# Strassen's block products for the projections of a hybrid decoder trunk on Trainium2

## The chip, the cores and the metric

The kernel runs on the 8 cores of one Trainium2 chip. Each core takes half of one of the four sequences (1024 tokens) and computes both layers for it alone; nothing is exchanged between cores. The time is the device time of the slowest core, in microseconds, as the median of three runs.

## The reference, cut to what matters

```python
xn = rms_norm(h, norm_g)
proj = xn @ w_in                       # (tokens, 2048) @ (2048, 15360)
a_in, a_b, a_c, a_z, b_in, b_z, c_val, c_gate, c_z, gates = split(proj)
y_a = a_b * causal_dwconv3(a_c * a_in) * silu(a_z)
y_b = groupwise(trailing_mean_w(b_in) - b_in) * pool_scale * silu(b_z)   # w = 2, 4, 8, 16
v   = causal_dwconv31(c_val * sigmoid(c_gate)) + conv_c_b
y_c = silu(layer_norm(v)) * silu(c_z)
merged = sum over n of sigmoid(gates[n]) * (y_n @ w_branch_out[n])       # (1024 -> 2048) each
h = h + merged @ w_o
h = h + sigmoid(h @ w_ple_gate) * (p @ w_ple_proj)
# two such layers, then a final rms_norm
```

## The kernel before, in words

Channels lie on the 128 partitions, tokens along the free axis: `h`, `xn`, `acc` are 16 rows of 128 channels, `yb` eight. A core holds 1024 tokens and 62 earlier ones (`HALO`), which the causal convolutions need; the ranges `R_in` and `R_out` shrink from layer to layer: 1086, 1056, 1056 and 1024 columns, in matmuls of 362, 352, 352 or 512 columns (`R_L`, L149).

All work is recorded by one scheduler (`Sched`), which puts a semaphore wait on an instruction for each tile that it depends on. Each engine executes its list in the order of recording. Every instruction is issued from L134, so the profile tells them apart by tile, not by line.

A weight group is 256 output channels, loaded by a POOL DMA that casts to bf16 into one of two buffers (`load_main`, L280). `mm_group` (L301) runs the 16 contraction steps for one half of a group (128 channels) over all columns and rotates through the eight PSUM banks. After each half, one ScalarE or VectorE instruction reads the whole result: sigmoid, silu or copy on ScalarE, a product or a sum on VectorE.

The stages of a layer, in order: sums of squares through a matmul with ones, and `xn`; gate and value of branch C, whose product goes to the upper rows of `h` (bitcast to bf16); branch A; `merge_branch(0)` (L361: two gate groups, then four output rows of 8 steps each, four times over); branch B; `merge_branch(1)`; branch C, where mean and variance come from matmuls with ones and `cz_norm` (L502) normalises a row; `merge_branch(2)`; the projection `w_o` into `h`; the gate `w_ple_gate`, followed in each of its eight groups by the small product with `p` and the update of `h`. Six rows of `h` are reloaded before `w_o`, from `xT` in layer 0 and from `h_keep` in layer 1.

The 31 taps of branch C's convolution, 248 VectorE instructions a layer, are kept in a queue; `bg(n)` (L236) records the next n of them after a projection, and what is left is recorded ahead of branch C. In the last layer the squares for the final norm are summed by matmuls with ones inside the gate stage.

Of the kernel before, what the change touches and what calls it, by code (L numbers as in the profile page):

```python
# [9 lines left out]
F32 = mybir.dt.float32  # L10
# [11 lines left out]
HALO = 62  # L22
TOK = 1024
TL = TOK + HALO
NCORES = 8
# [118 lines left out]
class Rng:  # L144
    def __init__(self, lo, n, nt):
        assert lo + n * nt == TL and n <= 512
        self.lo, self.n, self.nt = lo, n, nt

R_L = [  # L149
    (Rng(0, 362, 3), Rng(30, 352, 3)),  # L150
    (Rng(30, 352, 3), Rng(62, 512, 2)),
]
R_FINAL = Rng(62, 512, 2)
# [3 lines left out]

def build_program(depth_run=DEPTH):
    nc = bass.Bass("TRN2", target_bir_lowering=False)
# [10 lines left out]
    h_keep = nc.dram_tensor("h_keep", [6 * 128, TL], F32, kind="Internal").ap()  # L170
# [3 lines left out]
    dma_names = ["x0", "x1", "x2", "x3", "par", "p", "hw0", "hw1", "hw2", "hw3", "hw4", "hw5", "hr0", "hr1", "hr2", "hr3", "hr4", "hr5", "ring0", "ring1", "side0", "side1", "out0", "out1", "out2", "out3"]  # L174
# [4 lines left out]
    def TT(out, in0, in1, op, reads, writes):  # L179
        S.op("dve", "tensor_tensor", dict(out=out, in0=in0, in1=in1, op=op), reads, writes)  # L180

    def TS(out, in0, s1, s2, op0, op1, reads, writes):
        kw = dict(out=out, in0=in0, scalar1=s1, scalar2=s2, op0=op0)
        if op1 is not None:
            kw["op1"] = op1
        S.op("dve", "tensor_scalar", kw, reads, writes)

    def STT(out, in0, scalar, in1, op0, op1, reads, writes):
        S.op("dve", "scalar_tensor_tensor", dict(out=out, in0=in0, scalar=scalar, in1=in1, op0=op0, op1=op1), reads, writes)

    def RECIP(out, in_, reads, writes):
        S.op("dve", "reciprocal", dict(out=out, in_=in_), reads, writes)

    def MM(out, lhsT, rhs, start, stop, reads, writes):
        S.op("pe", "matmul", dict(out=out, lhsT=lhsT, rhs=rhs, start=start, stop=stop), reads, writes)

    def DMA(eng, out, in_, reads, writes, sem):
        S.op(eng, "dma_start", dict(out=out, in_=in_), reads, writes, dma_sem=sem)

    with ExitStack() as es:  # L200
# [12 lines left out]
        Tt = ec(nc.sbuf_tensor("Tt", [128, 6, TL], F32))  # L213
# [448 lines left out]
```

How the kernel before makes its waits and increments, by code:

```python
                def body(eng, ops=ops, e=e):  # L105
# [15 lines left out]
                            todo.append((key, val))  # L121
                        emb = None
                        if o.meth is not None and not o.is_dma:
                            for t in todo:
                                if t[0][0] == "e":
                                    emb = t
                            if emb is not None:
                                todo.remove(emb)
                        for key, val in todo:
                            sem = dma_sems[key[1]] if key[0] == "d" else sems[key[1]]
                            eng.wait_ge(sem, val)
                        if o.meth is None:
                            continue
                        ins = getattr(eng, o.meth)(**o.kw)
                        if emb is not None:
                            ins._wait_ge(sems[emb[0][1]], emb[1])
                        if o.is_dma:
                            ins.then_inc(dma_sems[o.dsem], 16)
                        elif o.signal:
                            ins.then_inc(sems[e], 1)
```

## Time and profile before

| | |
|---|---|
| median of three runs | 2729.83 us (2727.36 to 2809.83) |
| profiled execution | 2733.91 us, span 2732.3 us on the slowest core (2721.1 to 2732.3) |
| granted clock, mean of each core | 0.981 to 0.986 |
| busy, share of the span | TensorE 96%, weight loads 54%, VectorE 49%, ScalarE 13%, POOL 8% |
| matmuls | 15074 recorded |
| weights loaded by POOL's queue | 188.82 MB, 53.7% of the DMA engines' time |
| median from issue to landing of 1 MB of weights | 10.2 us (`w_in`), 10.6 us (`w_o`) |

The busy shares say which engine could set the time; the windows by stage say whether it does so in that stage. The engines are separate, so a busy engine costs time only where another waits for it, and within an engine an instruction that waits holds back all that are recorded behind it.

### The profile page before, as it was taken

Reading aid. Unit: us, or ns where it says so; the run is one execution under the profiler, and the core shown is the slowest. Engines: PE = TensorE matmul, PEld = TensorE weight load, DVE = VectorE, ACT = ScalarE, POOL = GpSimd, SP = SyncE. Lnnn points to the kernel's source line nnn. Section 1 sums busy time; section 2 is a strip of 40 time slices with the busy share of each in tenths; the row PEclk is TensorE's granted clock in tenths of the full one; section 3 lists DMA queues with packets and bytes.
Section 4 is the critical chain, followed back from the end, with each engine's and each line's share of the span. In section 5 each row is a group of like instructions: output and inputs, shape, how many; then the busy total and the mean of one; then the engine's idle time right before and its main releaser. Section 6 shows DMA issues by size and latency. Waiting matters only on the chain.

```text
span 2732.3 us, 33287 instructions; the slowest of 8 cores (2721.1 to 2732.3 us)
## 1 busy us (share of the span) xinstructions
PE 2620.0 (96%) x15074; PEld 1474.3 (54%) x15168; DVE 1336.4 (49%) x1107; ACT 358.0 (13%) x335; POOL 213.6 (8%) x206
## 2 busy tenths in 40 slices
PE   3999999999999999999979999999999999999994
PEld 1566666666666666666646655544554444444442
DVE  3476676555762531212255666756467434221135
ACT  1000001101101311011120000110111022101111
POOL 0000000001000000001100000000100000000110
PEclk7899999999999999999989999999999999999997
DMA  7465565455645565566555556555565556556654
GB/s 166 47 78 70 70 77 71 69 80 66 86 65 85 79 94 72 68 78 85 68 90 66 74 78 78 74 76 76 72 79 79 82 74 107 77 71 74 89 70 141
DMA packets 353198, 218.62 MB, mean 80 GB/s; under 512 B 4000, under 2 KB 346016, under 8 KB 353056
## 3 DMA queue, kind: packets, MB, share of 16 engines
q0 software_dynamic: 345760, 188.82, 53.7%
q1 hardware_dynamic: 7296, 27.67, 3.1%
q8 instruction: 119, 1.95, 0.3%
q14 instruction: 23, 0.19, 0.0%
HBM read 393.55 MB, written 11.72 MB: 148 GB/s over the span
## 4 chain that ended last, share of the span: by engine, by line
PE 92%; DVE 4%; DMA 3%; ACT 1%; issue 1%; SPq 0%; DVEq 0%; ACTq 0%; POOLq 0%
PE psa L134 92%; DVE xn L134 1%; DVE Tt L134 1%; DMA par_s<-par 1%; ACT Tt L134 1%; DMA ring<-w_in 1%; DMA icnt_s<-icnt 0%; DVE h L134 0%; DVE yb L134 0%; DMA outT<-Tt 0%; SPq L134 0%; DVEq L99 0%; ACT L134 0%; ACTq L131 0%; DVEq L131 0%
## 5 line engine op out<-in xcount | busy, mean ns | idle before, releaser
L134 PE MATMUL psa<-xn,ring 128*128 128x352 bf16 (+2 forms) x11459 | 1969.3, 332 | 36.0 <-DVE xn L134 24.2
L134 PEld LDWEIGHTS psa<-xn,ring 128*128 128x128 bf16 x11520 | 1119.3, 98 | 880.6 <-DVE xn L134 42.5
L134 DVE SCALAR_TENSOR_TENSOR h<-h,par_s 128x1056 f32<-128x1056 bf16 (+1 forms) x480 | 624.1, 1300 | 13.1
L134 DVE TENSOR_TENSOR Tt<-psa,Tt 128x1056 f32<-128x1056 f32 (+2 forms) x128 | 159.2, 1244 | 713.9 <-PE psa L134 713.9
L134 ACT ACTIVATE Tt<-psa 128x1056 f32<-128x1056 f32 (+2 forms) x224 | 233.5, 1042 | 1808.0 <-PE psa L134 1781.1
L134 PE MATMUL psa<-yb,ring 128*128 128x352 bf16 (+1 forms) x1902 | 342.3, 338 | 1.0
L134 POOL DMA_DIRECT2D ring<-w_in x120 | 137.4, 1145 | 1700.4 <-PE psa L134 1672.0
L134 PEld LDWEIGHTS psa<-yb,ring 128*128 128x128 bf16 x1920 | 186.5, 97 | 153.0
L134 PE MATMUL psa<-acc,ring 128*128 128x352 bf16 (+1 forms) x1269 | 226.0, 338 | 0.6
L134 PEld LDWEIGHTS psa<-acc,ring 128*128 128x128 bf16 x1280 | 124.2, 97 | 102.0 <-issue 0.3
L134 DVE TENSOR_TENSOR h<-psa,h 128x1056 f32<-128x1056 f32 (+1 forms) x32 | 39.7, 1241 | 183.9 <-PE psa L134 183.9
L134 DVE TENSOR_TENSOR Tt<-Tt 128x1056 f32<-128x1056 f32 (+9 forms) x60 | 75.7, 1261 | 81.1 <-ACT Tt L134 79.7
L134 DVE TENSOR_TENSOR acc<-psa,Tt 128x1056 bf16<-128x1056 f32 (+1 forms) x32 | 39.7, 1241 | 128.3 <-PE psa L134 128.3
L134 DVE TENSOR_TENSOR acc<-acc,Tt 128x1056 bf16<-128x1056 bf16 (+1 forms) x64 | 79.5, 1242 | 2.2
L134 PE MATMUL psa<-Tt,ones_s 128*128 128x352 bf16 (+2 forms) x166 | 41.7, 407 | 40.0 <-ACT Tt L134 30.8
L134 DVE TENSOR_TENSOR yb<-Tt 128x1056 bf16<-128x1056 f32 (+1 forms) x32 | 39.7, 1242 | 63.7 <-ACT Tt L134 63.7
L134 DVE TENSOR_TENSOR h<-psa,Tt 128x1086 bf16<-128x1086 f32 (+1 forms) x16 | 20.4, 1274 | 102.3 <-PE psa L134 102.3
L134 ACT ACTIVATE xn<-h 128x1056 bf16<-128x1056 f32 (+1 forms) x32 | 34.2, 1070 | 222.7 <-DVE h L134 222.7
L134 ACT ACT_TABLE_LOAD x21 | 26.9, 1283 | 210.1 <-PE psa L134 197.0
L134 PEld LDWEIGHTS psa<-Tt,ones_s 128*128 128x128 bf16 x168 | 18.1, 116 | 61.4 <-ACT Tt L134 34.0
L134 DVE TENSOR_TENSOR Tt<-h 128x1086 bf16<-128x1086 f32 (+4 forms) x32 | 34.9, 1116 | 30.7 <-DMA h<-xT 28.8
L134 DVE SCALAR_TENSOR_TENSOR xn<-h,par_s,Tt 128x1086 bf16<-128x1086 f32 (+1 forms) x32 | 40.0, 1331 | 16.3 <-ACT Tt L134 16.3
(33 smaller groups left out, 422.4 us busy)
## 6 DMA issues: line engine op xcount, KB each, us to landing
ring<-w_in POOLq DMA_DIRECT2D x120, 1024.0 KB, 10.2
ring<-w_branch_out POOLq DMA_DIRECT2D x24, 1024.0 KB, 9.2
ring<-w_o POOLq DMA_DIRECT2D x16, 1024.0 KB, 10.6
ring<-w_ple_gate POOLq DMA_DIRECT2D x16, 1024.0 KB, 10.7
h<-xT SPq DMA_DIRECT2D x4, 2172.0 KB, 22.5
outT<-Tt SPq DMA_DIRECT2D x16, 512.0 KB, 4.5
h<-xT SPq DMA_DIRECT2D x6, 543.0 KB, 4.9
h_keep<-h SPq DMA_DIRECT2D x6, 543.0 KB, 9.2
```

Of the source, the lines that this page charges most:

```text
L134: ins = getattr(eng, o.meth)(**o.kw)
```

## The change

Every projection over 16 row chunks is computed by one level of Strassen's algorithm in Winograd's form. Contraction, output channels and tokens are each cut in two. For a group of 256 channels, seven products of eight matmuls replace eight.

- Tokens are stored in two halves (`HL`), blocks of 16 tokens going to the halves in turn; the host reorders inputs and output. `HALO` becomes 64. A matmul has 272 or 256 columns, or 512 in layer 1's `R_out`.
- Sums of weight quarters: `prep_a` makes three on VectorE (one in place, over the weights), `prep_b` one more there and a copy on ScalarE. They are recorded inside the last unit of the group before, if the group after is a fast one. Sums of token halves: `make_T`, four VectorE instructions for each of `xn`, `acc` and the bf16 copy of `h`, written over `h` or `xn`.
- A fast unit holds four banks. `part0`: one product, copied by ScalarE to a second bank. `part1`: three products; the first is copied to `m7`. `add0` and `add1` are VectorE adds from PSUM to PSUM. `tail0`, `tail1`, `tail2`: three products, recorded inside the *next* unit, so that the reads of a result (`evac`) and what follows it (`after`) come there too.
- `run_units` records unit by unit. `bg` records convolution taps while a clock kept for VectorE (0.17 us + elements / 960) is behind one kept for TensorE; both start at 0, and the squares and `xn` at the start count for VectorE only.
- Plain as before: `w_branch_out`, `pool_w`, `w_ple_proj`, the LayerNorm sums, and the first groups of the `xn`, `w_o` and `w_ple_gate` stages.
- A third weight buffer lies in `h` during the `w_in` stages and in `acc` during the gate stage. As `h` is overwritten, all 16 rows are reloaded before `w_o`; layer 0 writes all of them to `h_keep`.
- Squares for the norms are summed by ScalarE (`Square`) and VectorE (`square_sum`), then by one step of matmuls. `icnt` gets a semaphore of its own.

```diff
-R_FINAL = Rng(62, 512, 2)
+R_L = [((0, 34), (1, 33)), ((1, 33), (2, 32))]
+
+def _subs(R):
+    b, n = R
+    if n == 32:
+        return [(b, 32)]
+    return [(b, 17), (b + 17, n - 17)]
...
+    def bg(limit, most):
+        n = 0
+        while bgq and n < most and clock["dve"] < limit:
+            bgq.popleft()()
+            n += 1
...
+        def prep_a(g):
+            g.sb = state["sb"]
+            state["sb"] ^= 1
+            q, r = g.slot.quads, r_sb[g.sb]
+            TT(sb_ap(g, 0), quarter(g, 1, 0), quarter(g, 1, 1), ALU.add, [q[2], q[3]], [r[0]], 2)
+            TT(quarter(g, 1, 0), quarter(g, 0, 0), quarter(g, 1, 0), ALU.subtract, [q[0]], [q[2]], 2)
+            TT(sb_ap(g, 1), sb_ap(g, 0), quarter(g, 0, 0), ALU.subtract, [r[0], q[0]], [r[1]], 2)
+
+        def prep_b(g):
+            q, r = g.slot.quads, r_sb[g.sb]
+            TT(sb_ap(g, 2), quarter(g, 0, 1), sb_ap(g, 1), ALU.subtract, [r[1], q[1]], [r[2]], 2)
+            ACT(sb_ap(g, 3), quarter(g, 1, 1), AF.Copy, [q[3]], [r[3]])
...
+        def fast_unit(g, X, R, evac, after=None, last=False):
+            b, n = R
+            N = n * 16
+            u = Unit(g, 56 * (N / 2400.0 + 0.0035), evac, after, last)
...
+            def part0():
+                b0, b1, b2, b3 = u.banks
+                for bk in (b1, b2):
+                    if bits[bk] < N:
+                        mm(bk, 512, ones[:, :], ones_wide, True, True, [r_ones])
+                rhs, rr = xq(0, 0)
+                prod(b0, wq(0, 0), g.slot.quads[0], rhs, rr, True, True)
+                ACT(psa[:, b1, 0:N], psa[:, b0, 0:N], AF.Copy, [r_bank[b0]], [r_bank[b1]])
+
+            def part1():
+                b0, b1, b2, b3 = u.banks
+                rhs, rr = tq(2)
+                prod(b3, wq(1, 0), g.slot.quads[2], rhs, rr, True, True)
+                ACT(m7[:, u.m, 0:N], psa[:, b3, 0:N], AF.Copy, [r_bank[b3]], [r_m7[u.m]])
+                rhs, rr = xq(1, 0)
+                prod(b0, wq(0, 1), g.slot.quads[1], rhs, rr, False, True)
+                rhs, rr = tq(1)
+                prod(b1, sq(1), r_sb[g.sb][1], rhs, rr, False, True)
+
+            def add0():
+                b0, b1, b2, b3 = u.banks
+                TT(psa[:, b2, 0:N], psa[:, b1, 0:N], m7[:, u.m, 0:N], ALU.add, [r_bank[b1], r_m7[u.m]], [r_bank[b2]])
+
+            def tail0():
+                rhs, rr = tq(0)
+                prod(u.banks[1], sq(0), r_sb[g.sb][0], rhs, rr, False, True)
+
+            def add1():
+                b0, b1, b2, b3 = u.banks
+                TT(psa[:, b3, 0:N], psa[:, b1, 0:N], m7[:, u.m, 0:N], ALU.add, [r_bank[b1], r_m7[u.m]], [r_bank[b3]])
+
+            def tail1():
+                rhs, rr = tq(3)
+                prod(u.banks[2], sq(3), r_sb[g.sb][3], rhs, rr, False, True)
+
+            def tail2():
+                rhs, rr = xq(1, 1)
+                prod(u.banks[1], sq(2), r_sb[g.sb][2], rhs, rr, False, True)
...
+                        prep_a(u.group)
+                        prep_b(u.group)
+                    u.part0()
...
+                        evac(o, 0)
+                        bg(base + 0.55 * u.cost, 3)
+                        o.tail1()
+                        u.part1()
+                        o.tail2()
+                    else:
+                        u.part0()
+                        bg(base + 0.55 * u.cost, 3)
+                        u.part1()
+                release(u)
+                prep = prep and nxt.slot is not None
+                if prep:
+                    prep_a(nxt)
+                if o is not None:
+                    evac(o, 1)
+                if prep:
+                    prep_b(nxt)
+                state["old"] = u if u.fast else None
+                if not u.fast:
+                    for i in range(len(u.pieces)):
+                        evac(u, i)
+                look_ahead()
+                bg(clock["pe"], 4)
+            if state["old"] is not None:
+                finish(state["old"])
...
+        def square_sum(k, R, sq, r_sq, tot, r_tot):
+            src = ab(row(F_h, k), R)
+            if k == 0:
+                ACT(ab(tot, R), src, AF.Square, r_h[k], r_tot)
+                return
+            ACT(ab(sq, R), src, AF.Square, r_h[k], r_sq)
+            if k < 15:
+                TT(ab(tot, R), ab(tot, R), ab(sq, R), ALU.add, r_tot + r_sq, r_tot)
+            else:
+                TT(ab(view(ttb, 4 * 2 * TL, [[1, TL]]), R), ab(tot, R), ab(sq, R), ALU.add, r_tot + r_sq, r_T[4])
...
+                def pool():
+                    for c in range(2):
+                        src, r_src = Tt[:, c, :], r_T[c]
+                        lo, sh, st = R_in[0] * 32, 1, 0
+                        while sh < wlen:
+                            dst, r_dst = Tt[:, 2 + st % 2, :], r_T[2 + st % 2]
+                            lo += sh
+                            TT(dst[:, lo:TL], src[:, lo:TL], src[:, lo - sh:TL - sh], ALU.add, r_src, r_dst)
+                            src, r_src = dst, r_dst
+                            sh *= 2
+                            st += 1
...
+                    def norm():
+                        for c in range(2):
+                            i = 2 * j + c
+                            v = view(F_V, i * TL + LO, [[1, TL - LO]])
+                            TT(tmp[:, LO:TL], v, mu[:, LO:TL], ALU.subtract, [r_V[i]] + r_mu, r_tmp)
+                            TT(tmp[:, LO:TL], tmp[:, LO:TL], rstd[:, LO:TL], ALU.mult, r_tmp + r_rstd, r_tmp)
+                            ACT(tmp[:, LO:TL], tmp[:, LO:TL], AF.Silu, r_tmp + [r_par], r_tmp, bias=pcol(PB + 48 + i), scale=pcol(PB + 40 + i))
+                            TT(ab3(row(F_yb, i), R_out), tm3(tmp, R_out), ab3(row(F_T, s + c), R_out), ALU.mult,
+                               r_tmp + r_T[s + c], [r_yb[i]])
...
+                def ln():
+                    sl = slice(LO, TL)
+                    TT(tmp[:, sl], mu[:, sl], mu[:, sl], ALU.mult, r_mu, r_tmp)
+                    TT(rstd[:, sl], rstd[:, sl], tmp[:, sl], ALU.subtract, r_rstd + r_tmp, r_rstd)
+                    TS(rstd[:, sl], rstd[:, sl], 0.0, LN_EPS, ALU.max, ALU.add, r_rstd, r_rstd)
+                    ACT(rstd[:, sl], rstd[:, sl], AF.Ln, r_rstd, r_rstd)
+                    ACT(rstd[:, sl], rstd[:, sl], AF.Exp, r_rstd, r_rstd, scale=-0.5)
+                    n0()
+
...
+                    def gated(p, c=c):
+                        TT(P_ab(F_P, 2, p), P_ps(p), P_ab(F_P, c, p), ALU.mult, P_res(p) + r_P[c], r_P[2])
+
+                    def upd(oc=oc):
+                        TT(ab(row(F_h, oc), R_out), ab(row(F_h, oc), R_out), ab(row(F_P, 2), R_out), ALU.add, r_h[oc] + r_P[2], r_h[oc])
+                        if not last_layer:
+                            DMA("sp", h_keep[oc * 128:(oc + 1) * 128, :], h[:, oc, :], r_h[oc], [r_keep[oc]], f"hw{oc}")
```

In the gate stage a group's units are followed by two plain units (output rows c = 0 and 1), whose reads are `gated` and whose `after` is `upd`. In branch B the `after` of the first group is `pool`; in branch A the product `c_in` is followed by `conv3` (six VectorE instructions). In branch C the units in order are: the first z group, the mean (ahead of it the rest of the taps), the variance with `ln` as its `after`, three z groups with `norm`.

## Rows read from the trace of the kernel before

**Rows 1.** The page: busy by engine, the granted clock, the chain that ended last.

```profile
PE 2620.0 (96%) x15074; PEld 1474.3 (54%) x15168; DVE 1336.4 (49%) x1107; ACT 358.0 (13%) x335; POOL 213.6 (8%) x206
...
PEclk7899999999999999999989999999999999999997
...
PE 92%; DVE 4%; DMA 3%; ACT 1%; issue 1%; SPq 0%; DVEq 0%; ACTq 0%; POOLq 0%
```

**Rows 2.** Windows by stage: stretch, length, engines' busy us, clock, DMA share, GB/s.

```profile
101.20:427.90 326.70, 326.70 (x2112) 206.68 (x2113) 218.76 (x174) 23.70 (x22) 23.98 (x21) 0.99 0.56 71
601.10:729.20 128.10, 125.92 (x819) 78.82 (x817) 80.88 (x78) 18.30 (x17) 13.16 (x13) 1.00 0.55 71
902.40:970.20 67.80, 65.20 (x433) 41.77 (x432) 39.06 (x34) 26.01 (x23) 4.57 (x4) 1.00 0.57 87
1258.90:1394.40 135.50, 132.61 (x865) 82.78 (x864) 37.23 (x31) 19.11 (x19) 15.38 (x16) 1.00 0.61 86
1932.80:2055.40 122.60, 120.16 (x666) 65.06 (x673) 77.08 (x76) 17.89 (x17) 12.83 (x13) 1.00 0.58 73
2564.40:2696.00 131.60, 130.35 (x592) 58.45 (x604) 43.57 (x37) 24.82 (x24) 12.28 (x14) 1.00 0.51 64
```

**Rows 3.** Timeline of TensorE: start, length, instructions merged; merges of both layers.

```profile
471.21 29.03 PE L134 MATMUL psa<-xn,ring 128*128 128x352 bf16 x192
500.08 1.22 PE L134 MATMUL psa<-yb,ring 128*128 128x352 bf16 x7
...
1808.05 27.88 PE L134 MATMUL psa<-xn,ring 128*128 128x512 bf16 x126
1835.77 0.60 PE L134 MATMUL psa<-yb,ring 128*128 128x512 bf16 x2
```

**Rows 4.** Groups by form: count | busy us, mean ns of one | idle before, releaser.

```profile
L134 PEld LDWEIGHTS psa<-xn,ring 128*128 128x128 bf16 x11520 | 1119.3, 98 | 880.6 <-DVE xn L134 42.5 <-issue 9.8 <-DVE Tt L134 2.5
...
L134 DVE SCALAR_TENSOR_TENSOR h<-h,par_s 128x1056 f32<-128x1056 bf16 x232 | 305.6, 1317 | 6.3
...
L134 ACT ACTIVATE Tt<-psa 128x1056 f32<-128x1056 f32 x112 | 117.6, 1050 | 927.2 <-PE psa L134 900.4 <-DVE h L134 26.8
...
L134 DVE TENSOR_TENSOR Tt<-psa,Tt 128x1056 f32<-128x1056 f32 x64 | 80.4, 1256 | 368.0 <-PE psa L134 368.0
...
L134 DVE TENSOR_SCALAR Tt<-Tt,par_s 128x1056 f32<-128x1056 f32 x8 | 6.4, 801 | 0.3
...
L134 DVE TENSOR_TENSOR Tt<-h 128x1056 bf16<-128x1056 bf16 x4 | 2.7, 706 | 0.3 <-PE psa L134 0.2
L134 DVE TENSOR_TENSOR tmp<-Tt,icnt_s 128x16 f32<-128x16 f32 x16 | 2.7, 168 | 0.0
```

**Rows 5.** Timeline of ScalarE at the start, as rows 3.

```profile
51.02 1.17 ACT L134 ACTIVATE Tt<-psa,par_s 128x1086 f32<-128x1086 f32 x1 [11.31 <-DMA icnt_s<-icnt]
```

**Rows 6.** Windows around TensorE's wait for the third weight load, as rows 2.

```profile
98.00:101.20 3.20, 0.01 (x1) 0.05 (x2) 3.17 (x3) 0.00 (x0) 1.14 (x1) 0.83 0.33 41
101.20:103.00 1.80, 1.80 (x7) 0.90 (x8) 1.73 (x3) 0.00 (x0) 0.00 (x0) 0.50 1.39 117
103.00:106.00 3.00, 3.00 (x12) 1.49 (x11) 2.93 (x3) 0.00 (x0) 0.00 (x0) 0.50 0.86 84
```

**Rows 7.** Timeline of TensorE in layer 0's gate stage, two periods.

```profile
1292.71 14.61 PE L134 MATMUL psa<-xn,ring 128*128 128x352 bf16 x96
...
1309.65 1.53 PE L134 MATMUL psa<-xn,ring 128*128 128x352 bf16 x9
```

**Rows 8.** Timeline of ScalarE behind the variance, layer 0.

```profile
930.48 2.20 ACT L134 ACTIVATE Tt<-Tt 128x1056 f32<-128x1056 f32 x2 [4.44 <-DVE Tt L134]
932.70 1.28 ACT L134 ACT_TABLE_LOAD   x1
934.00 1.27 ACT L134 ACTIVATE Tt<-Tt,par_s 128x1056 f32<-128x1056 f32 x1
```

**Rows 9.** The page's DMA issues: KB each, median us to landing.

```profile
h<-xT SPq DMA_DIRECT2D x6, 543.0 KB, 4.9
```

More of the change, by code:

```diff
@@ new lines, in build_program, with load_ready @@
+        bits = [0] * 8
+        queue = deque()
+        units = []
+        groups_seen = set()
+        def load_ready():
+            while queue:
+                g = queue[0]
+                pick = next((f for f in free if f.phase is None or f.phase == g.phase), None)
+                if pick is None:
+                    return
+                free.remove(pick)
+                queue.popleft()
+                g.slot = pick
+                hold = r_h[11] if state["loads"] < 3 else []
+                state["loads"] += 1
+                if g.kind == "bo":
+                    dst = view(pick.ap, 0, [[512, 8], [1, 512]])
+                else:
+                    dst = view(pick.ap, 0, [[256, 16], [1, 256]])
+                DMA("pool", dst, g.src.rearrange("(k p) c -> p k c", p=128), hold, pick.quads, pick.sem)
@@ L296, in load_side @@
+        def load_side(g):
             s = state["side"]
             state["side"] ^= 1
[L298 to L308 removed]
@@ new lines, in build_program, with mm, add_unit @@
+        ones_wide = view(ones[:, :], 0, [[0, 4], [1, 128]])
+        def mm(bank, n, lhsT, rhs, start, stop, reads):
+            if start:
+                bits[bank] = n
+            S.op("pe", "matmul", dict(out=psa[:, bank, 0:n], lhsT=lhsT, rhs=rhs, start=start, stop=stop, skip_group_check=True),
+                 reads, [r_bank[bank]])
+        def add_unit(u):
+            units.append(u)
+            g = u.group
+            if g.kind in ("w", "bo") and id(g) not in groups_seen:
+                groups_seen.add(id(g))
+                queue.append(g)
+            return u
@@ new lines, in evac, with next_set, whole, finish @@
+        def evac(u, i):
+            u.evac(u.pieces[i])
+            if i == len(u.pieces) - 1 and u.after is not None:
+                u.after()
+        def next_set():
+            st = state["set"]
+            state["set"] ^= 4
+            return st
+        def whole(u):
+            u.place(next_set())
+            u.part0()
+            u.part1()
+            for i in range(len(u.pieces)):
+                evac(u, i)
+        def finish(o):
+            o.tail0()
+            o.add1()
+            evac(o, 0)
+            o.tail1()
+            o.tail2()
+            evac(o, 1)
+            state["old"] = None
```

842 lines of the change are left out of this document (499 added, 343 removed).

## The prediction

> **What bounds the kernel now.** I read the page first, then the spans by stage, then the order of instructions inside a stage. The page's shares and its chain of waits [rows 1] say that TensorE sets the time: it is busy for 96% of the span, holds 92% of the chain that ended last, and its granted clock stands at full speed in nearly every slice. The windows by stage [rows 2] say the same stage by stage: in the projections of layer 0 TensorE fills the whole stretch, in the pooling stage, the LayerNorm stage and the gate of the per-layer embedding all but 2 to 3 us. VectorE is busy for two thirds of the first stretch and a quarter to a half of the others, so today it is late nowhere for long. In the timeline of TensorE [rows 3] 192 products of 352 columns take 28.87 us from start to start (150.4 ns each) and 128 of 512 columns 27.72 us (216.6 ns): the columns at 2.4 GHz plus 3.5 ns. A weight group (256 output rows, 16 chunks) costs 14.43 us in layer 0 and 13.86 us at 512 columns.
>
> **The change, part by part.** All sums are against the profiled execution: span 2732.3 us, 2733.9 with what lies around it, 4.1 us above the median of the runs shown.
>
> *Columns.* 72 of each layer's weight groups become seven block products of eight matmuls. A group with two pieces of 272 and 256 columns costs 56 x (116.8 + 110.2) ns = 12.7 us, one of 512 columns 56 x 216.6 ns = 12.1 us: 1.7 us less each, 144 groups, **-248 us**. The branch outputs, the small projections and the first groups of three stages stay whole. The new matmuls are short; a weight load takes 98 ns here [rows 4], and no row shows one under fewer than 352 columns. I take it as hidden, since 98 is below 110; if half of the 52 ns between today's loads is needed too, 124 ns would stand against 110 to 117, some 10 ns in 10,080 short products: 0 to 100 us. The Trainium skill (TensorE: Matmul & The Clock Gate, section LDWEIGHTS) puts a load at its columns over 1.2 GHz, an estimate of 107 ns for 128; the row has 98, and by the one as by the other the sum stays, with 3 or 12 ns to spare.
>
> *Other work taken away.* The 32 matmuls that sum squares in the last gate stage go (7 us). The start no longer waits 11.3 us for icnt [rows 5] but gains a chain of squares and adds: -6. Two groups share the first pass over xn, whose rows come from VectorE every 1.3 us: -12 over both layers. A third weight buffer removes the 3.2 us gap and the clock at half level, 1.2 GHz, behind it [rows 6]: -5. The gaps in the five stages with side products or LayerNorm, 2 to 3 us of idle TensorE each [rows 2], and the filling of their short products go: -17. So if TensorE never waited longer than today: 2732 - 248 - 7 - 40 = **2437 us**.
>
> *What it adds to VectorE.* By size, VectorE costs 0.16 us + 1.04 ns a column, bf16 alone half the slope (706 ns at 1056); ScalarE 0.17 us + 0.84 ns [rows 4]. Added: 576 weight sums (0.69 us), 468 adds in PSUM (0.44 us at 272 columns, 0.69 at 512; no row has PSUM on both sides: lower bound this, upper bound twice it), 24 sums of tokens (2.4 us), some 80 more by split reads. That is 400 + 235 + 58 + 50 us on top of 1336: some 75% of the time, where it had 49%. The order of work matters more: a fast unit's last two products, and so its result, come only at the end of the *next* unit, and everything behind them on the in-order engines moves too. I follow five places; a product of eight matmuls is 0.93 us (1.73 at 512), its result is readable 0.26 us later.
>
> 1. *Gate of the per-layer embedding.* Now a period is 16.9 us [rows 7]. New, layer 0, from the end of the last gate unit: second sigmoid at 4.4; then on VectorE, in this order, the two gated reads 5.9, update of h 7.1, square on ScalarE 8.2, add to the running sum 9.6, weight sums 11.7 and 12.4, second gated read 13.9, update 15.1, square 16.2, add 17.5. The next group's second product needs the second weight sum (11.0), and ScalarE's copy of its first product stands behind the second square (16.6). After that TensorE still has 2 + 1 + 1 + 3 + 2 products: 24.8 us a period where its own work is 14.5. Cost 7 for the first and 6 x 10.3: **69 us**. Layer 1, counted the same way: 23.6 against 13.9, **65 us**.
> 2. *Pooling.* The pooled sums (2.6 us a level, 3.5 fixed: 6 to 14 us) can start only after the following unit, and the PSUM add of that unit queues behind them on VectorE. TensorE covers 5.4 us in layer 0, 3.5 in layer 1, where the pooling product itself waits: 30 + 28 us; the side products ahead of the next group's weight sums cost 2 us each, 17: **75 us**.
> 3. *LayerNorm of branch C.* Now the chain table load, Ln, Exp, table load, Silu [rows 8] runs under the next projections. New, the weight sums of the next group are issued *behind* that chain and both normalised rows: 18.8 us on VectorE and ScalarE, in which TensorE has one product. 19 + 18 us. The three later norms hold ScalarE's copies: 5.4 and 3.6 us each, 16 + 11. Squares through one buffer: 4 + 4. The planner also spreads 248 taps (1.32 us) by its own clock: in layer 0 it counts VectorE's start-up (50 us) as a lead, 50 + 410 of other work + 315 of taps = 775 us against 757 of TensorE, so 13 taps are left for the drain: 15 after what covers it. **86 us**.
> 4. *Three-tap convolution.* 6.9 us on VectorE (TENSOR_SCALAR 0.80, two of 1.32, twice [rows 4]) ahead of the next PSUM add; TensorE covers 5.4 and the lag of a tap adds 1.5. Layer 0 only, since at 512 columns it covers 10: **18 us**.
> 5. *Smaller.* First weight sums behind a branch output's reads in merges: 24 places, **29 us** (0 to 45). w_o: the bf16 copies of h stand ahead of ScalarE's copy, and two buffers for a load: **14 us** (0 to 30). The end: the last square is added on VectorE: **4 us**. The reload of h, 16 rows where 6 took 4.9 us each [rows 9], is counted at nothing: it runs under the last merge's final 14 us and the first three w_o groups (40 us); without that cover the ten late rows would cost 49 us, less what is left of it.
>
> *Clock.* After the 3.2 us gap the granted clock was 0.50, 1.2 GHz, for some 5 us [rows 6], 2.5 us lost. Places 2 to 4 make 15 gaps of that size: **37 us** (0 to 60).
>
> Sum: 2437 + 69 + 65 + 75 + 86 + 18 + 29 + 14 + 4 + 37 = 2834 us of span; 4.1 off and 1.6 on for the median: **2830 us**, 3.7% slower.
>
> **The rivals.** *A. TensorE stays the bound (faster).* Place 1 is the decider: if VectorE and ScalarE, a quarter idle or more, clear their queues before TensorE reaches the wait, only part of the 397 us is paid. For it: 248 us of columns are certain, TensorE has nothing else to wait for, and VectorE's idle time now is 1396 us. Against it: these waits are in the order of issue, not in the sum of work. With at most half paid: 2437 + 140 to 200, about **2600 us**; it wins wherever less than 240 us is paid. *B. Only the long chains hold (no change).* Places 1 to 3 without clock and small places: 2437 + 295 = **2732 us**. *C. VectorE becomes the bound of the first half (much slower).* Up to the drain it has some 775 us of work in layer 0 to TensorE's 750. If a PSUM add costs 0.9 us, 184 adds before it put 80 us more there, and as much again in layer 1: **2950 us**. It decides from 0.6 us an add. *D. The short products expose the weight load:* 2437 + 100 us and less waiting, since TensorE is later itself: about 2840, inside the forecast's range.
>
> **How the numbers follow.** A measurement tells 2% from no change here, 55 us. Forecast 0.46, D 0.05, A 0.25, B 0.18, C 0.06. The forecast's own range is 2760 to 2910 (chains 10% shorter or longer, small places at their bounds). The range reaches into A as far as half of it: 2620; above, to 2920. Faster by over 2%: A, 0.25. Within 2%: B and the lower edge of the forecast, 0.18 + 0.04. Slower: the rest of the forecast, C and D, 0.42 + 0.06 + 0.05 = 0.53.
>
> **What would show it.** TensorE's busy time near 2370 us and its count near 16,700. In the gate stages periods of 23 to 25 us, with TensorE waiting on VectorE's weight sums and on ScalarE's copy; if the period is below 18, A holds. One TensorE gap of 15 to 20 us a layer behind the variance product. In the pooling stage gaps that grow by 2.5 us from group to group. Weight loads of 98 ns with TensorE without gaps in the merges, where a group should take 12.7 us; 14 would be D. A PSUM add above 0.6 us would be C. The forecast is wrong if these waits together hold under 300 us.

## The result, and the profile after

The changed kernel took 2862 and 2867 us against 2727 to 2730 us before: ratio **1.0498 [1.0452, 1.0544]**, 5.0% slower, where 2830 us and 3.7% were forecast. In some runs cores ran long stretches at a lower granted clock; the slowest such runs are left out of the ratios, e5 and e8 are also compared by core 0 (its mean span over the runs in the ratio), and e7 is read by its undisturbed stages. The profiled execution took 2867.18 us, its span is 2865.6 us, 133.3 more than before.

The page after (busy by engine, granted clock in 40 slices, the chain that ended last), which answers to [rows 1]:

```profile
PE 2435.2 (85%) x16704; PEld 1649.2 (58%) x16704; DVE 2002.9 (70%) x2342; ACT 725.5 (25%) x1109; POOL 215.6 (8%) x206
...
PEclk9999999998997899998779999999999989999887
...
PE 65%; DVE 22%; ACT 5%; issue 5%; DMA 2%; SPq 0%; DVEq 0%; ACTq 0%; POOLq 0%
```

TensorE lost 185 us of busy time and gained 318 us of idle time. A quarter of the chain now belongs to VectorE and ScalarE, and yet neither is full. The windows by stage (length, busy us, clock), which answer to [rows 2]: first stretch, a merge, pooling, LayerNorm and gate of layer 0, then pooling, LayerNorm and gate of layer 1:

```profile
79.00:380.20 301.20, 288.37 (x2457) 240.75 (x2455) 242.53 (x321) 78.54 (x153) 27.57 (x23) 0.98 0.71 78
380.20:547.10 166.90, 159.56 (x1403) 136.03 (x1401) 148.18 (x170) 40.20 (x76) 11.79 (x11) 1.00 0.68 76
547.10:698.90 151.80, 121.55 (x973) 97.61 (x971) 113.83 (x156) 38.31 (x73) 12.93 (x13) 0.91 0.58 67
865.40:988.70 123.30, 77.16 (x583) 60.16 (x581) 83.31 (x93) 37.45 (x54) 5.45 (x5) 0.81 0.34 43
1265.80:1467.00 201.20, 141.51 (x1018) 107.50 (x1016) 91.68 (x116) 50.41 (x82) 13.07 (x14) 0.80 0.53 88
...
1952.50:2099.60 147.10, 120.05 (x716) 70.53 (x714) 113.33 (x143) 35.13 (x55) 12.92 (x13) 0.91 0.63 68
2259.50:2360.20 100.70, 69.97 (x286) 28.78 (x284) 60.17 (x65) 33.81 (x36) 5.50 (x6) 0.85 0.46 52
2636.40:2826.50 190.10, 132.61 (x509) 51.42 (x507) 86.34 (x88) 45.73 (x52) 10.75 (x12) 0.88 0.32 41
```

Stage by stage, in both traces (lengths in us; the cost is what the waits and the clock took, that is the difference plus the columns saved at 1.7 us a group and the small gaps that were there before). The w_o and gate stages are taken from first product to first product (in the changed kernel 1153.12, 1263.13 and 2521.85, 2633.79), the others from the windows, whose edges lie 1 to 8 us beside the first product of a stage:

| stage | before | after | cost, both layers | forecast |
|---|---|---|---|---|
| start, first stretch, change of layer, tail | 836.1 | 746.6 | 11 for the three-tap convolution | 18 |
| merges (three a layer) | 1018.8 | 977.6 | 42 | 29 |
| pooling | 128.1 + 122.6 | 151.8 + 147.1 | 80 | 75 |
| LayerNorm | 67.8 + 64.0 | 123.3 + 100.7 | 111 | 86 |
| w_o | 115.5 + 112.3 | 110.0 + 111.9 | 18 | 14 |
| gate | 135.5 + 131.6 | 203.9 + 192.7 | 164 | 134 |
| clock, forecast as a term of its own | | | in the rows above | 37 |

Pooling, LayerNorm and gate gave back more than the others won. (In the gate's 164 us are the 7 us of matmuls that went; the waits of LayerNorm's third norm, 5.39 and 4.29 us, stand in the merges' row.) The prices by form (count | busy us, mean ns), which answer to [rows 4]: the weight load, the PSUM add at two widths, a weight sum:

```profile
L135 PEld LDWEIGHTS psa<-h,sums 128*128 128x128 bf16 x4608 | 455.3, 99 | 200.3 <-DVE psa L135 21.2 <-issue 8.9
...
L135 DVE TENSOR_TENSOR psa<-psa,m 128x272 f32<-128x272 f32 x216 | 96.3, 446 | 148.6 <-PE psa L135 148.3
...
L135 DVE TENSOR_TENSOR psa<-psa,m 128x512 f32<-128x512 f32 x108 | 75.2, 696 | 162.4 <-PE psa L135 162.2
L135 DVE TENSOR_TENSOR ring<-ring 128x1024 bf16<-128x1024 bf16 x108 | 74.7, 692 | 3.7
```

They are near the forecast's (99 ns, 0.45, 0.70 and 0.69 us), so rival C falls. The merge, the second of the windows above, holds eight weight groups and four sets of branch outputs (14.5 us each by their columns): at 12.7 us a group that makes 8 x 12.7 + 4 x 14.5 = 159.6 us, and TensorE was busy for 159.56, so D, with 14 us a group, falls too. In the gate stage of layer 0 TensorE waits twice a period, first for the weight sums, then for ScalarE's copy of the first product (timeline of TensorE: start, length, idle before and its releaser):

```profile
1309.47 1.65 PE L135 MATMUL psa<-xn,acc 128*128 128x272 bf16 x8 [4.69 <-DVE acc L135]
1314.91 1.99 PE L135 MATMUL psa<-Tt,acc 128*128 128x272 bf16 x8 [3.79 <-ACT psa L135]
...
1336.59 1.46 PE L135 MATMUL psa<-xn,ring 128*128 128x272 bf16 x8 [4.68 <-DVE ring L135]
1342.03 2.00 PE L135 MATMUL psa<-Tt,ring 128*128 128x272 bf16 x8 [3.98 <-ACT psa L135]
```

These are the two waits of the forecast's place 1. The period is 1336.59 - 1309.47 = 27.1 us, where [rows 7] had 16.9 and the forecast 24.8. Windows of one such period say where the 2.3 us more are:

```profile
1305.00:1309.40 4.40, 0.00 (x0) 0.00 (x0) 3.22 (x5) 2.03 (x2) 0.00 (x0) 1.00 1.23 201
1309.40:1311.50 2.10, 1.65 (x8) 0.87 (x8) 2.03 (x5) 0.00 (x0) 0.00 (x0) 0.61 0.42 146
1311.50:1315.00 3.50, 0.09 (x1) 0.09 (x2) 2.26 (x3) 1.51 (x3) 0.00 (x0) 0.50 0.21 88
1315.00:1318.50 3.50, 3.50 (x16) 2.30 (x17) 0.86 (x1) 0.17 (x1) 0.00 (x0) 0.50 0.19 76
...
1322.00:1336.00 14.00, 9.37 (x82) 7.54 (x79) 5.56 (x8) 4.53 (x7) 1.87 (x2) 1.00 0.78 89
```

Behind the waits the granted clock is 0.50, 1.2 GHz, and a product of 272 columns lasts 1.65 to 2.0 us instead of 1.1. In LayerNorm of layer 0 the timeline of TensorE shows the drain, the wait of place 3 and the three norms:

```profile
899.82 1.06 PE L135 MATMUL psa<-h,ones_s 128*128 128x264 bf16 x4 [15.10 <-DVE h L135]
...
929.25 1.99 PE L135 MATMUL psa<-h,ring 128*128 128x272 bf16 x8 [15.79 <-DVE ring L135]
...
955.37 1.89 PE L135 MATMUL psa<-xn,ring 128*128 128x256 bf16 x8 [5.38 <-ACT psa L135]
...
994.97 1.89 PE L135 MATMUL psa<-xn,ring 128*128 128x256 bf16 x8 [5.39 <-ACT psa L135]
```

The forecast had 15, 19 and three of 5.4 us. ScalarE's chain [rows 8] is the same as before; what is new is that the weight sums stand behind it.

### The profile page after: what moved, and what is told of

It reads as the page before. It is cut to its first block, busy times and chain, and to the rows that moved or that the text cites. A ratio compares the mean times of both kernels' runs of the same rounds, so it can differ in the third digit from the quotient of the medians.

```text
span 2865.6 us, 39498 instructions; the slowest of 8 cores (2847.9 to 2865.6 us)
## 1 busy us (share of the span) xinstructions
PE 2435.2 (85%) x16704; PEld 1649.2 (58%) x16704; DVE 2002.9 (70%) x2342; ACT 725.5 (25%) x1109; POOL 215.6 (8%) x206
## 4 chain that ended last, share of the span: by engine, by line
PE 65%; DVE 22%; ACT 5%; issue 5%; DMA 2%; SPq 0%; DVEq 0%; ACTq 0%; POOLq 0%
PE psa L135 65%; DVE h L135 7%; DVE Tt L135 6%; DVE sums L135 3%; ACT Tt L135 2%; DVE acc L135 2%; ACT acc L135 1%; DVE psa L135 1%; DVE xn L135 1%; DVE ring L135 1%; DMA ring<-w_o 1%; DMA h<-xT 1%; DVE yb L135 1%; DMA outT<-Tt 0%; ACT psa L135 0%
## 5 line engine op out<-in xcount | busy, mean ns | idle before, releaser
L135 PE MATMUL psa<-h,sums 128*128 128x272 bf16 (+2 forms) x4608 | 705.4, 303 | 12.9 <-DVE psa L135 12.8
L135 PEld LDWEIGHTS psa<-h,sums 128*128 128x128 bf16 x4608 | 455.3, 99 | 200.3 <-DVE psa L135 21.2
L135 PE MATMUL psa<-xn,ring 128*128 128x272 bf16 (+2 forms) x3008 | 471.3, 304 | 70.0 <-DVE ring L135 35.7
L135 DVE TENSOR_TENSOR psa<-psa,m 128x272 f32<-128x272 f32 (+2 forms) x468 | 233.3, 499 | 420.9 <-PE psa L135 414.1
L135 PE MATMUL psa<-xn,sums 128*128 128x272 bf16 (+2 forms) x2544 | 422.0, 313 | 40.6 <-DVE psa L135 40.6
L135 ACT ACTIVATE Tt<-psa 128x544 f32<-128x544 f32 (+2 forms) x312 | 220.8, 708 | 837.0 <-PE psa L135 524.1
L135 PEld LDWEIGHTS psa<-xn,ring 128*128 128x128 bf16 x3008 | 297.3, 100 | 194.5 <-DVE ring L135 39.6
L135 PEld LDWEIGHTS psa<-xn,sums 128*128 128x128 bf16 x2544 | 255.3, 101 | 165.3 <-DVE psa L135 47.9
L135 PE MATMUL psa<-yb,h 128*128 128x256 bf16 (+2 forms) x1536 | 235.0, 310 | 13.7 <-ACT Tt L135 13.7
L135 PE MATMUL psa<-h,ring 128*128 128x272 bf16 (+2 forms) x1104 | 175.0, 302 | 39.6 <-DVE ring L135 39.4
## 6 DMA issues: line engine op xcount, KB each, us to landing
ring<-w_in POOLq DMA_DIRECT2D x88, 1024.0 KB, 12.7
```

What stands on the lines that cost most here:

```text
L135: ins = getattr(eng, o.meth)(**o.kw)
```

## The experiments

The theory: the time is lost in the order of issue on the in-order engines, behind the deferred tails, and in the half clock behind each such wait. The rivals: VectorE has too much work; the block products themselves are not worth their columns. All ratios are to the kernel before, measured beside it.

**e1: weight sums ahead of side products.**

```diff
-nxt = next((v.group for v in units if v.group is not u.group), None) if u.last else None
+nxt = next((v.group for v in units if v.group is not u.group and v.group.kind in ("w", "bo")), None) if u.last else None
```

> The work of every engine is the same; only the weight sums of the next weight group are issued earlier: in the last unit of the block-product group before, ahead of the side products and of the units of ones that lie between. Theory (the time is lost in the order of issue behind the deferred tails): a period of the gate stage loses the four sums that stand between its two gated reads, 2.8 us: 27.2 to about 24.5 us in layer 0, some 20 us a layer; the one TensorE wait a side product in pooling goes (8 us together), the 15.8 and 15.1 us waits behind the variance product shrink by 1 to 4 us only, because ScalarE's copy of the first product still stands behind the normalisation. Sum about 2815 us. Rival (the amount of VectorE work is the bound, its 2003 us at 70%): nothing was taken away, so 2865 us, periods still 27 us.

Measured: 2817 to 2827 us, ratio 1.0337 [1.0318, 1.0357]. VectorE's busy time is unchanged, 1999.8 us. In the gate stage the first wait is gone and the second has grown by less (timeline of TensorE, one period of 24.2 us):

```profile
1307.71 2.00 PE L135 MATMUL psa<-Tt,acc 128*128 128x272 bf16 x8 [6.54 <-ACT psa L135]
...
1331.88 2.00 PE L135 MATMUL psa<-Tt,ring 128*128 128x272 bf16 x8 [6.09 <-ACT psa L135]
```

That is 43 us for a change of order alone, where the rival of amount expected none.

**e2: dummy products in the gate's waits, first try.** Products of ones into the unit's next bank (`b3`) ahead of its first product from weight sums, and more of them (into `b2`) ahead of the product from `sums`.

> In the block-product groups 2 to 7 of the gate stages TensorE runs dummy products of ones (512 columns) where it waits: 20 and 15 of them a period in layer 0 (4.3 and 3.2 us for waits of 4.7 and 3.5 to 4.3), 15 and 10 in layer 1. Theory that the half clock behind these waits lengthens the period beyond the 24.8 us of the forecast: granted clock 1.00 through the period, products behind the waits 0.93 instead of 1.8 to 2.0 us, period 27.2 to 24.8 us in layer 0, about 1.2 us less in layer 1; together 20 to 25 us, 2842 us. Rival (the clock costs nothing because the waits behind it absorb it): clock 1.00, the waits longer by what the products gain, period still 27 us, 2865 us.

Measured: ratio 1.0629 [1.0592, 1.0667], slower. I had put the second batch behind the product that waits for ScalarE's copy, so it filled nothing; it ran at half clock and was added to the period, and the wait of 4.34 us left ahead of it still put the product behind it at 2.00 us (timeline of TensorE):

```profile
1316.60 2.00 PE L135 MATMUL psa<-Tt,acc 128*128 128x272 bf16 x8 [4.34 <-ACT psa L135]
1318.39 5.13 PE L135 MATMUL psa<-ones_s 128*128 128x512 bf16 x15
```

It says nothing on the question; e6 asks it again.

**e3: the gate's groups whole.**

```diff
-g = Group(w_pg[l][:, q * 256:(q + 1) * 256], "w", ph + 2, q > 0)
+g = Group(w_pg[l][:, q * 256:(q + 1) * 256], "w", ph + 2, False)
-    fast_group(g, X_h, R_out, sg)
+    plain_group(g, hrow, R_out, sg)
```

> The 14 block-product groups of the two gate stages are whole products again (the rest of the change stays). Theory (place 1 of the sum: the order of issue in these stages): periods back at about 17 us, the stages at 140 and 134 us instead of 201 and 190, so about 115 us less: 2750 us. Rival (amount of VectorE work): only 14 x 4 sums and 21 x 2 adds go, some 55 us of VectorE work, so at most 55 us less. Rival (nothing is lost here, block products cost little more than whole ones): TensorE has 25 us more columns to pass, so slower, 2890 us.

Measured: 2740 to 2743 us, 1.0042 [1.0026, 1.0058]: some 123 us less than the changed kernel, with 60 us less VectorE work (1942.7). A period is 16.7 us again. More than the amount rival's bound of 55 us came back, so the block products of place 1 alone made the difference between slower and no change.

**e4: e1, and the squares on the background queue.**

```diff
-square_sum(oc, R_out, row(F_P, 3), r_P[3], row(F_P, 4), r_P[4])
+bgq.append(lambda: square_sum(oc, R_out, row(F_P, 3), r_P[3], row(F_P, 4), r_P[4]))
```

> As e1, and in the gate stages the square and the add to the running sum of squares are no longer issued in the update of h but put on the queue of background work, which is issued behind ScalarE's copies of the next block-product group. All work is kept. Theory (order of issue): between the last sigmoid and the next group's copy VectorE has two gated reads and two updates, 5.4 us instead of 14; a period of about 18.5 to 20 us in layer 0 (TensorE's own 14.5 plus a wait of some 4), 18 in layer 1; gate stages about 147 and 140 us, together with the rest of e1 some 120 us less than after: 2745 us. Rival (amount of VectorE work): 2865 us, periods still above 26 us.

Measured: 2766 to 2777 us, 1.0157 [1.013, 1.0184], 20 to 30 us above the expectation: the adds to the running sum now stood ahead of the PSUM add, and TensorE waited for that (core 1; the next period has the same wait):

```profile
1306.53 1.10 PE L135 MATMUL psa<-xn,sums 128*128 128x272 bf16 x8 [3.58 <-DVE psa L135]
```

**e5: the squares behind the PSUM add.** As e4, but the closures go to a queue of their own that is emptied at the end of a block-product unit; even rows square into `F_T` row 4.

```diff
+while late and u.fast:
+    late.popleft()()
 look_ahead()
 bg(clock["pe"], 4)
```

> As e4, but the square and the add to the running sum are issued at the end of the next block-product unit, behind its PSUM add (in e4 they stood ahead of that add, and TensorE waited 3.6 us a period for it in layer 0 and 2.3 us in layer 1; even and odd rows get a buffer each). Theory (order of issue): that wait goes, and the half clock behind it; period about 16.5 to 17.5 us in layer 0 (e4: 20.5 to 22.2) and 15 to 15.5 in layer 1 (e4: 17.7); 50 us less than e4: 2720 us. Rival (amount of VectorE work): same work as e4, same 2770 us.

Measured: ratio 1.0085 [1.0019, 1.015]; the slowest core took 25 us or more above the expected 2720. Core 0's span, as a mean, is 2716.9 us, where e1 has 2814.7 and e4 2762.8: 46 us less than e4, where 50 were expected. In the gate stage of layer 0 a period is 15.8 us and the longest wait 0.5:

```profile
1317.02 1.10 PE L135 MATMUL psa<-xn,sums 128*128 128x272 bf16 x8 [0.43 <-DVE psa L135]
...
1332.78 1.10 PE L135 MATMUL psa<-xn,sums 128*128 128x272 bf16 x8 [0.43 <-DVE psa L135]
```

From 27.1 to 15.8 us with the same 1999 us of VectorE work: in layer 0 the order was nearly the whole of place 1. Layer 1's period is 17.6 us, where 15 to 15.5 were expected: two waits of 1.2 us stay.

**e6: the dummies in the right place, on the changed kernel.**

```diff
+for _ in range(u.warm[0]):
+    mm(b3, 512, ones[:, :], ones_wide, True, True, [r_ones])
 rhs, rr = tq(2)
 prod(b3, ...)
...
+for _ in range(u.warm[1]):
+    mm(b2, 512, ones[:, :], ones_wide, True, True, [r_ones])
 rhs, rr = xq(1, 0)
 prod(b0, ...)
```

> The test of the clock again, on the changed kernel itself, with the second dummies at their proper place: e2 put them behind the product that waits for ScalarE's copy, where they only added columns; here they stand ahead of it. 20 and 16 products of ones a period in layer 0 (4.3 and 3.5 us, in waits of 4.7 and 3.5 to 4.3), 15 and 10 in layer 1. Theory that the half clock behind the waits is what lengthens the period from the forecast's 24.8 to 27.2 us: granted clock 1.00 throughout, the three products behind the waits 0.93 us each instead of 1.8 to 2.0, period 24.8 in layer 0, about 1.2 us less in layer 1; together about 25 us: 2840 us. Rival (the waits are set by VectorE and ScalarE from a point that the clock does not move): period still 27 us, 2865 us.

Measured: 2832 to 2854 us, 1.0399 [1.0345, 1.0453]. The timeline of TensorE:

```profile
1329.99 1.10 PE L135 MATMUL psa<-xn,acc 128*128 128x272 bf16 x8 [0.37 <-DVE acc L135]
1330.93 3.62 PE L135 MATMUL psa<-ones_s 128*128 128x512 bf16 x16
1335.43 1.10 PE L135 MATMUL psa<-Tt,acc 128*128 128x272 bf16 x8 [0.89 <-ACT psa L135]
...
1354.58 1.10 PE L135 MATMUL psa<-xn,ring 128*128 128x272 bf16 x8 [0.37 <-DVE ring L135]
```

The window of this period, then one of the changed kernel's (length, TensorE, weight loads, VectorE, ScalarE, POOL, clock):

```profile
1329.99:1354.58 24.59, 22.80 (x164) 15.71 (x165) 12.12 (x17) 6.80 (x11) 1.87 (x2) 1.00 0.51 93
```

```profile
1309.47:1336.59 27.12, 18.11 (x129) 13.60 (x129) 12.13 (x17) 6.79 (x11) 1.87 (x2) 0.81 0.51 84
```

With TensorE kept at work the granted clock of this period is 1.00 and it lasts 24.59 us with the same work on VectorE and ScalarE; in layer 1 a period lasts 23.5 (TensorE's products behind ScalarE's copy start at 2729.65 and 2753.15). Those are the forecast's 24.8 and 23.6. So the chain of place 1 was counted rightly, and half clock is the rest. The dummies cover six periods a layer, (2.5 + 2.3) x 6 = 29 us, and the shorter runs, 2832 and 2836 us, are that much below the changed kernel's.

**e7: convolution and pooled sums in halves.** As e1; `conv3` and `pool` for one row chunk each, the second called between `add1` and the first read of the next group's first unit; z in two units in layer 1.

```diff
 o.add1()
+if o.mid is not None:
+    o.mid()
 evac(o, 0)
```

> As e1, and the three-tap convolution and the pooled sums are issued in two halves, one row chunk each: the second half stands behind the second PSUM add of the next group's first unit instead of ahead of it; in layer 1 the z groups of the pooling stage run as two units of 256 columns, so that they have a next unit to cover the halves. The work is the same. Theory (places 2 and 4: a long VectorE block ahead of a PSUM add): the four 2.8 us waits in layer 0's first stretch go (11 us); the waits of 1.9, 4.4, 7.2 and 9.8 us of layer 0's pooling fall to 4 us in all and those of layer 1 (3.5 to 10 us, 24 us in all) by half; with some half clock given back 40 to 50 us less than e1: 2775 us. Rival (amount of VectorE work): 2819 us, the waits only move.

Measured: ratio 1.0445 [1.0366, 1.0525]; nothing was won where 40 to 50 us were expected. The last pooling group of layer 0 had one wait of 9.78 us for VectorE and now has two that come to 10.07 (timeline of TensorE, first the changed kernel's, then e7's):

```profile
691.86 2.00 PE L135 MATMUL psa<-xn,sums 128*128 128x272 bf16 x8 [9.78 <-DVE psa L135]
```

```profile
681.26 1.10 PE L135 MATMUL psa<-xn,sums 128*128 128x272 bf16 x8 [2.85 <-DVE psa L135]
689.57 1.89 PE L135 MATMUL psa<-h,sums 128*128 128x256 bf16 x8 [7.22 <-DVE psa L135]
```

Between the two adds TensorE has one product of 1.1 us, which I had not counted, while VectorE has the second half of the sums: cutting a block in two does not shorten the chain from the last product of u to the first product that needs z's second add. The convolution's waits went from 2.80 to 3.16 us, for its read instead of its add. In places 2 and 4 halves did not help; the waits still grow from group to group with the length of the sums, as in the changed kernel (1.88, 4.52, 7.17 and 9.78 us).

**e8: LayerNorm's rows in pieces, planner level.** As e1; `norm` cut in a VectorE part and a ScalarE part, which go to a queue that is emptied behind the next units' copies and PSUM adds, and

```diff
 X_xn.make_T(R_in)
+if l == 0:
+    clock["dve"] = clock["pe"]
```

> As e1, and in LayerNorm's stage (place 3) the rows are normalised in pieces behind ScalarE's copies of the next block-product units, not in one block ahead of them (logarithm and exponential behind the first copy, then a row's subtraction and product at the end of one unit, its Silu and last product in the next); besides, the planner that spreads the convolution taps starts layer 0 with VectorE's clock equal to TensorE's, so that no taps are left over. The work is the same. Theory (order of issue): layer 0's waits of 17.8 (drain), 12.5, 4.6, 5.2 and 5.4 us fall to 5 us in all, layer 1's of 11.3 and three of 3.9 to 3 us; with 10 us of half clock given back about 70 us less than e1: 2750 us. Rival (VectorE is full in layer 0's first half): the drain's 15 us come back as waits between 80 and 900 us, and only about 45 us are won.

Measured: 1.0159 [1.0114, 1.0203]; core 0's span, as a mean, is 2752.7 us against 2814.7 in e1: 62 us, between the theory's 70 and the rival's 45. The drain's wait (17.76 us in e1) is gone, the one behind the variance is 2.51 us where e1 had 12.52 and the changed kernel 15.79, and the norms' are 0.4 to 1.9 in layer 0; in layer 1 one of 4.43 stays:

```profile
904.25 1.69 PE L135 MATMUL psa<-h,sums 128*128 128x272 bf16 x8 [2.51 <-DVE psa L135]
914.65 1.10 PE L135 MATMUL psa<-xn,ring 128*128 128x272 bf16 x8 [0.44 <-ACT psa L135]
```

One new wait of 6.21 us for VectorE stands at 90.95, where the taps now begin; the rest of the drain did not come back, which the rival expected (TensorE's waits between 60 and 890 us come to 49 us, in e1 to 43).

**e9, e10, e11: the orders together; whole products in the three stages; the orders without whole products in pooling.** e9 is e1 + e5 + e8 with pooling's u and z groups whole (each row chunk pooled right after its product), e10 has the gate, pooling and LayerNorm groups whole and no new order, e11 is e9 with pooling as in e1.

> The changed kernel with the orders that helped, and the pooling stage put back: weight sums ahead (e1), squares behind the PSUM add (e5), LayerNorm's rows in pieces and taps by a planner that starts level (e8; here with 6 us of lead, since e8 had a new wait of 6.2 us at its first block products), and the u and z groups of the pooling stage whole again, each row chunk pooled right after its product. Theory (order of issue): 110 us from the gate stages (e1 to e5), 70 us from LayerNorm (e1 to e8), 45 us from pooling (152 and 147 us back to some 128 and 123) below e1's 2819: about 2600 us, 5% under the kernel before. Rival (VectorE's amount of work is the bound): with its 2000 us kept it stays near 2720.

> The changed kernel with the block products kept only where TensorE waits little (first stretch, merges, w_o) and all weight groups whole in the three stages of places 1 to 3 (gate, pooling, LayerNorm); no new order besides. Theory (order of issue behind deferred tails): these stages go back to nearly their lengths of before: 125 us from the gate (e3), 48 from pooling, 77 from LayerNorm (drain of 15 us kept): 2867 - 250 = about 2615 us. Rival (the waits move on to the other stages): above 2700 us. Rival of size (block products in the three stages are worth their 64 us of columns): then e9 lies well below it.

> As e9, but the pooling stage stays in block products as in the changed kernel (with the weight sums ahead). Theory: 45 us more than e9, 2645 us, with waits of 1.9, 4.4, 7.2 and 9.8 us in layer 0's pooling as in e1; rival (pooling whole costs its columns, 27 us, and gains nothing): as fast as e9 or faster.

Measured: e9 2664 to 2671 us, **0.9762 [0.9748, 0.9775]**; e10 2661 to 2667, 0.9750 [0.9731, 0.9770]; e11 2667 to 2673, 0.9774 [0.9757, 0.9790] (the ratios rest on five, two and three runs). All three took more than expected, by 67, 49 and 25 us. Two things follow. e11's page has the same 16704 products and practically the VectorE work of the changed kernel in 195 us less time:

```profile
PE 2384.6 (89%) x16704; PEld 1630.8 (61%) x16704; DVE 1997.3 (75%) x2342; ACT 734.2 (27%) x1117; POOL 215.2 (8%) x206
```

and e10, which does without 64 us of saved columns, is as short: in the three stages together these orders pay back what block products save and no more. That does not hold for every order and stage: e11's pooling still has the waits of 1.88 to 9.79 us, and layer 0's gate in e5's order has a shorter period (15.8 us) than whole products (16.7). And pooling whole won some 4 us (e9 against e11) where 45 were expected. In e10, as in e9, TensorE waits anew for VectorE's read of the side product (first TensorE, then VectorE):

```profile
661.64 0.64 PE L135 MATMUL psa<-xn,ring 128*128 128x272 bf16 x2 [4.90 <-DVE yb L135]
```

```profile
648.77 12.15 DVE L135 SCALAR_TENSOR_TENSOR h<-h,par_s 128x1056 f32<-128x1056 bf16 x9
660.84 3.05 DVE L135 SCALAR_TENSOR_TENSOR yb<-psa,par_s,Tt 128x512 bf16<-128x512 f32 x4
```

Nine taps, 12.2 us, stand ahead of that read. Is it order again, or simply VectorE's work?

**e12: no taps ahead of the side product's read.** e10, with the gate of layer 0 in block products in e5's order, and

```diff
+ahead = bool(units) and units[0].group.kind == "side"
...
-bg(base + 0.55 * u.cost, 3)
+if u.group.kind != "side" and not ahead:
+    bg(base + 0.55 * u.cost, 3)
...
-bg(clock["pe"], 4)
+if not ahead:
+    bg(clock["pe"], 4)
```

> As e10 (weight groups of pooling, LayerNorm whole, pool of each row chunk right behind its product), with three edits: the gate stage in block products in layer 0 alone, in e5's order (squares behind the PSUM add, weight sums ahead); no convolution taps are issued ahead of a side product's read, in the unit before it or in its own first half (in e9 and e10 TensorE waits 4 to 5.5 us a group for that read, eight times, and ahead of it VectorE has 9 to 11 taps of 1.33 us). Theory (order of issue: these waits are taps in front of the read): the eight waits go, about 30 us of them, at most 15 us come back as leftover taps at layer 0's drain; the gate stage of layer 0 gains 7 us: 2625 to 2640 us. Rival (VectorE is full in the pooling stage and the merges around it, 85 to 88% busy): the taps only move, the waits with them: 2655 us.

Measured: 2607 to 2614 us, **0.9559 [0.9540, 0.9578]**, 4.4% faster than the kernel before. In the same group VectorE now waits for TensorE, and TensorE for nothing (VectorE, then TensorE):

```profile
635.49 5.37 DVE L135 SCALAR_TENSOR_TENSOR h<-h,par_s 128x1056 f32<-128x1056 bf16 x4
643.06 3.05 DVE L135 SCALAR_TENSOR_TENSOR yb<-psa,par_s,Tt 128x512 bf16<-128x512 f32 x4 [2.19 <-PE psa L135]
```

```profile
642.12 2.19 PE L135 MATMUL psa<-Tt,side 128*128 128x256 bf16 x16
644.15 6.04 PE L135 MATMUL psa<-xn,ring 128*128 128x272 bf16 x48
```

and the page reads:

```profile
PE 2415.7 (93%) x17078; PEld 1668.3 (64%) x17078; DVE 1879.0 (72%) x2124; ACT 655.9 (25%) x984; POOL 215.3 (8%) x206
...
PEclk9999999999999999999989999999999999999997
```

The taps did not come back at the drain (the wait there is 1.5 us, as in e10). The gain over e10 was 52 us where 24 to 39 were expected. Three things came at once. The profiles of core 0 lie 71.5 us apart: 27.5 ahead of layer 0's w_o, 9.4 in its w_o and gate, 34.6 in layer 1 (on core 6, e12's slowest: 20, under 1 and 27). Waits of 34 us for that read, seven of 4 to 6 us in e10, are gone, all outside the gate, so the order of the taps gave most of the gain. What the weight sums ahead, the later squares and the granted clock (0.980 to 0.986 against e10's 0.975 to 0.978) gave beside it is not separated.

## Why the prediction was right or wrong

**Right: the sign and the places.** The column gain came (a merge group takes 12.7 us, weight loads 99 ns, no wait for them there), and the idle time that it bought, 318 us more, came mostly where the five places put it. e1, e3, e5 and e8 took the waits of places 1 and 3 away one by one, and the time followed: 43, 123, and by core 0's spans 98 and 62 us (e5 and e8 against e1). VectorE's amount was no bound in the stages whose order was changed: its work is the same in e11, which is 195 us shorter. Rival A needed the queues to clear before TensorE came to the wait; in the forecast's order they did not, but e5 shows for layer 0's gate that they could (longest wait 0.5 us).

**Wrong: "Clock. ... Places 2 to 4 make 15 gaps of that size: 37 us".** That step left out place 1, whose 14 periods hold the same kind of wait twice each. In layer 0 the period is 27.1 us; at full clock (e6) it is 24.6, and in layer 1 it averages 25.8 against 23.5, so seven periods a layer would make (2.5 + 2.3) x 7 = 34 us that the term did not hold. The sum of busy time says the same: the forecast had TensorE busy for 2370 us and 37 more by the clock; the page has 2435.2, so slow products cost about 65 us and not 37. That is 28 of the 32 us by which the profiled span lies above the forecast's 2834. The other 3 to 4 are waits: TensorE was idle for 430 us, where the forecast makes 2834 - 2370 - 37 = 427.

**The smaller terms.** That the waits came out right in sum is luck in part.

- Place 2 by the forecast's own figures (levels of 2.6 us, 3.5 fixed, less 5.4 or 3.5) makes 18 and 26 us, not 30 and 28; the four waits of layer 0 came to 23.4, those of layer 1 to 16.3.
- Place 4 by its own figures is 6.9 - 5.4 + 1.5 = 3.0 us a wait, 12 and not 18; four of 2.80 came.
- Place 3 had 13 taps left for the drain; 15 were (20.3 us).
- Merges took 42 us, where 29 stood for the weight sums, but not for that reason: those cost about 1 us in five places of layer 0. 9.7 of the 42 are the third norm of place 3, and some 20 are waits for ScalarE ahead of the branch outputs (twelve of 0.53 us in layer 0 and of 1.18 in layer 1), which the forecast did not name.
- w_o took 18 us for 14, and half of it is one wait in layer 1 for a weight load, issued at 2542.80 when a buffer came free (timeline of TensorE):

```profile
2553.14 3.15 PE L135 MATMUL psa<-acc,ring 128*128 128x512 bf16 x7 [9.42 <-DMA ring<-w_o]
```

**Right for a thinner reason than given.** Place 2 was argued from the length of the pooled sums. The waits do grow with it, but e7 shows that issuing the sums in halves does not shorten them: what counts is all that VectorE does between the last product of u and the first that needs z's second add. What e12 did in the stage with whole products, moving taps, was not tried with the stage in block products.

## What to carry to other kernels

When a change shortens the bounding engine and hands results out later, do not compare sums of work: write down, stage by stage, what stands in each in-order queue between the last late result and the next thing the bounding engine needs. Use the cheaper form where that distance is covered, and leave the old form where it is not; here the whole products in three stages beat the cheaper ones in their first order by 200 us. A better order can bring the cheaper form back, as in layer 0's gate (a period of 15.8 us against 16.7 whole). And count the clock for every wait in the list: here two waits of some 4 us cost 2.5 us more behind them.

## What the hardware showed beside

- After waits of 4.7 and 3.8 us, with one product between them, the clock stood at 0.50, 1.2 GHz, from 1311.5 to 1318.5 us; with dummy products in the same waits (e6) it stayed at 1.00 and the period was 2.5 us shorter, though TensorE did 36 matmuls of 512 columns more.
- In e7's profile the granted clock was 0.81 through the last merges of both layers on all cores that I read, with TensorE 98 to 99% busy (windows, core 0):

```profile
1000.00:1050.00 50.00, 49.51 (x367) 39.50 (x365) 19.41 (x29) 9.63 (x18) 3.15 (x3) 0.81 0.67 80
```

  The Trainium skill (TensorE: Matmul & The Clock Gate, section "Seeing it yourself") states that a die goes to 13/16 of its clock once three of its cores run dense matmuls. By that the merges would show 0.81 in every profile. The changed kernel shows 1.00 in its merge from 380 to 547 us, with eight cores at the same work and TensorE busy for 159.56 of 166.90 us, and also from 1000 to 1050 us (busy for 49.23). And where 0.81 came in other profiles it came on two cores of a die and not on the other two: on cores 6 and 7 in e5 (2300 to 2400 us, the others 1.00), on cores 0 and 1 in e6 (1000 to 1120 us; cores 2 and 3 had 1.00). So the page's rule does not hold as it stands here, and the measurement decides; what sets the 0.81 off stays open.
- A load of `w_in` took 12.7 us from issue to landing (median) in the changed kernel and 12.0 to 14.7 in the variants, 10.2 before, for the same bytes. With the third buffer more loads can be under way at once, which may be the reason; no run tests it.
